# A decoder layer on one NeuronCore: the first unit of either feed-forward network reordered on three engines, and the last tile of the first down projection done bank by bank

## The reference

```python
h = swiglu(rms_norm(x, ffn1_pre_g), w_gate, w_up, w_down)     # 2048 -> 5632 -> 2048
x = x + 0.5 * rms_norm(h, ffn1_post_g)
u = rms_norm(x, mix_pre_g)                                    # one input projection
a, m = mla_attention(...), moba_attention(...)                # 8 heads each
y = concat[rms_norm(a), rms_norm(m)] @ w_out
x = x + rms_norm(y, mix_post_g)
x = x + 0.5 * rms_norm(swiglu(rms_norm(x, ffn2_pre_g), ...), ffn2_post_g)
# swiglu(x) = (silu(x @ w_gate) * (x @ w_up)) @ w_down
```

## Time and profile before

| | |
|---|---|
| median of three runs | 1758.3 us |
| profiled execution: own time / span of its instructions | 1758.18 / 1756.5 us |
| PE busy | 1737.1 us, 99% (7968 matmuls) |
| PEld busy | 1442.3 us, 82% |
| DVE busy | 1410.7 us, 80% |
| ACT busy | 1001.8 us, 57% |
| POOL busy | 65.3 us, 4% |
| granted TensorE clock, mean | 0.998 |

### The profile page before, as it was taken

How to read it: one execution, slowest core, us unless ns; L and a number is a source line. 1 busy time by engine, 2 the same in 40 slices (tenths; PEclk the granted TensorE clock), 3 DMA queues, 4 the chain that set the end, 5 groups by cost and what they waited for, 6 DMA issues and landing times. The chain is left out here.

```text
span 1756.5 us, 21394 instructions
## 1 busy us (share of the span) xinstructions
PE 1737.1 (99%) x7968; PEld 1442.3 (82%) x7968; DVE 1410.7 (80%) x1284; ACT 1001.8 (57%) x979; POOL 65.3 (4%) x99
## 2 busy tenths in 40 slices
PE   9999999999999999999999999999999999999998
PEld 8788888888888888788888878788888888888886
DVE  7888888888888888765578558888888888888887
ACT  6666565555655654543347446555666666555563
POOL 1000000000000000010000000000000000000000
PEclk9999999999999999999999999999999999999999
DMA  9777777777766554355441546777777777666453
GB/s 386 237 257 259 256 256 239 239 239 248 245 234 222 184 215 176 147 219 189 174 162 54 187 171 260 263 240 241 249 249 241 239 246 251 254 232 238 174 191 114
DMA packets 58978, 389.75 MB, mean 222 GB/s; under 512 B 6432, under 2 KB 6688, under 8 KB 16160
## 3 DMA queue, kind: packets, MB, share of 16 engines
q1 hardware_dynamic: 52720, 344.77, 50.1%
q0 software_dynamic: 6048, 44.04, 13.2%
q10 hardware_dynamic: 144, 0.04, 0.0%
HBM read 384.63 MB, written 4.19 MB: 221 GB/s over the span
## 5 line engine op out<-in xcount | busy, mean ns | idle before, releaser
L2093 PE MATMUL banks<-w_hi,act_hi 128*128 128x512 f32 (+1 forms) x1088 | 424.7, 390 | 1.1 <-DVE act_lo L1355 1.1
L2095 PE MATMUL banks<-w_hi,act_lo 128*128 128x512 f32 (+1 forms) x1088 | 421.5, 387 | 0.0
L2094 PE MATMUL banks<-w_lo,act_hi 128*128 128x512 f32 (+1 forms) x1088 | 421.2, 387 | 0.0
L1385 DVE TENSOR_TENSOR op_lo<-quads,op_hi 128x2048 fp32r<-128x2048 f32 x140 | 318.5, 2288 | 43.2 <-ACT op_hi L918 42.8
L918 ACT ACTIVATE op_hi<-quads 128x2048 fp32r<-128x2048 f32 x140 | 266.8, 1919 | 53.3 <-PE banks L2095 21.1
L2287 PE MATMUL banks<-w_hi,hid_split 128*128 128x512 f32 x992 | 275.1, 389 | 0.5 <-DVE hid_split L1616 0.5
L1374 DVE TENSOR_TENSOR w_lo<-raw,w_hi 128x2048 fp32r<-128x2048 f32 x80 | 181.3, 2287 | 78.3 <-ACT w_hi L892 78.3
L1344 DVE TENSOR_TENSOR w_lo<-raw,w_hi 128x2048 fp32r<-128x2048 f32 (+3 forms) x67 | 143.8, 2147 | 121.6 <-ACT w_hi L843 121.6
L2093 PEld LDWEIGHTS banks<-w_hi,act_hi 128*128 128x128 f32 x1088 | 204.6, 188 | 42.1 <-issue 1.8
L2095 PEld LDWEIGHTS banks<-w_hi,act_lo 128*128 128x128 f32 x1088 | 204.4, 188 | 41.7
L2094 PEld LDWEIGHTS banks<-w_lo,act_hi 128*128 128x128 f32 x1088 | 204.6, 188 | 40.0
(11 more groups left out here) (209 smaller groups left out, 2329.8 us busy)
## 6 DMA issues: line engine op xcount, KB each, us to landing
raw<-in_weights SPq DMA_DIRECT2D x203, 1024.0 KB, 5.1
quads<-in_paired SPq DMA_DIRECT2D x80, 1024.0 KB, 10.7
quads<-in_paired POOLq DMA_DIRECT2D x40, 1024.0 KB, 8.5
raw<-in_paired SPq DMA_DIRECT2D x32, 768.0 KB, 5.9
rows<-in_x SPq DMA_DIRECT2D x4, 1024.0 KB, 10.9
raw<-in_weights SPq DMA_DIRECT2D x6, 512.0 KB, 3.5
gain_row<-in_post_gains SPq DMA_DIRECT2D x3, 1024.0 KB, 6.6
raw<-in_weights SPq DMA_DIRECT2D x4, 768.0 KB, 4.1
```

What stands on the lines that cost most here:

```text
L1385: nc.vector.tensor_tensor(op_lo[:, slot, :], op_raw(op), op_hi[slot][:, :], ALU.subtract)\
L2093: nc.tensor.matmul(out_ap, hi, rhs_hi, start=start, stop=False, skip_group_check=chain)
L2094: nc.tensor.matmul(out_ap, hi, rhs_lo, start=False, stop=False, skip_group_check=chain)
L2095: return nc.tensor.matmul(out_ap, lo, rhs_hi, start=False, stop=stop, skip_group_check=chain)
```

## The change

In unit 1 of both layers, and only there:
- DVE does `multiply_hidden(stage, 1, 1)` after the low part of P6, no more ahead of `sum3`; the two joins of part1 come ahead of the low part of L4; `multiply_mixed` comes ahead of the low part of the next unit's L1.
- ACT does `keep_hidden(stage, 1, 1)` after the kept P7 and the high part of P5; the kept P5 comes ahead of the high part of L4.
- PE turns block 1 after P6, no more ahead of P7.

At the end of `DOWN1` PE does tile 1 of the last piece bank by bank: six matmuls into the first bank, a semaphore (`near_bank_done`), six into the second. ACT squares the two banks apart, in two instructions of 512 columns, so there is one more sum, one more step of the variance on POOL, and the later counts go up by one (16 to 17, 26 to 27, 28 to 29).

```diff
@@ POOL, inverse_rms
+                        if job == R_POST1 and n == parts - 1 and t == TILES - 1:
+                            sums[0] += 1
+                            pool.wait_ge(squared, sums[0])
+                            step(nc.gpsimd.tensor_scalar(var[:, job, one], sumsq[:, one, parts], c / width,
+                                                         var[:, job, one], ALU.mult, ALU.add))
@@ ACT, unit
-                keep_hidden(stage, 1 if v.first else u * 2 - 2, u * 2 - 1)
-                keep_part(stage, v, part1[:, 1, :], O_P7)
-                operand_high(stage, v, O_P5)
+                if v.first:
+                    keep_part(stage, v, part1[:, 1, :], O_P7)
+                    operand_high(stage, v, O_P5)
+                    keep_hidden(stage, 1, 1)
+                else:
...
                 keep_part(stage, v, part0[:, 1, :], O_P6)
                 operand_high(stage, v, O_P2)
-                plain_high(stage, v, L4)
-                keep_part(stage, v, part1[:, 0, :], O_P5)
+                if v.first:
+                    keep_part(stage, v, part1[:, 0, :], O_P5)
+                    plain_high(stage, v, L4)
+                else:
...
@@ ACT, in place of square_down(DOWN1, 1)
+            def square_end(stage):
+                act.wait_ge(tile0_done, DP)
+                b = down_banks(1, 0)
+                square(banks[:, b:b + 2, :].rearrange("p b n -> p (b n)"), junk[:, 0:D // 2], 0, 1)
+                act.wait_ge(near_bank_done, 1)
+                square(banks[:, down_banks(1, 1), :], junk[:, 0:BANK], 1, 1)
+                act.wait_ge(piece_used, stage + DP)
+                square(banks[:, down_banks(1, 1) + 1, :], junk[:, 0:BANK], 1, 2)
@@ DVE, unit
                 operand_low(stage, v, O_P6)
+                if v.first:
+                    multiply_hidden(stage, 1, 1)
...
-                plain_low(stage, v, L4)
+                if not v.first:
+                    plain_low(stage, v, L4)
                 dve.wait_ge(part_kept, per_unit(stage, u, 4, 4))
                 join_part(part1, 1, part1[:, 0, :])
                 dve.wait_ge(op_used, per_unit(stage, u, 3, OP_COUNT[O_P3]))
                 join_part(part1, 0, banks[:, Y_BANK, :], ALU.subtract)
+                if v.first:
+                    plain_low(stage, v, L4)
                 operand_low(stage, v, O_P4)
                 mix_block(stage, u, part1, 2, L2, 2, ALU.subtract)
-                if not last:
+                if v.first:
+                    multiply_mixed(stage, u * 2, part1, per_unit(stage, u, 4, 1))
                     plain_low(stage, unit_behind(v), L1)
-                multiply_mixed(stage, u * 2, part1, per_unit(stage, u, 4, 1))
...
@@ DVE, ahead of unit 1
-                multiply_hidden(stage, 1, 1)
                 sum3(stage, v)
@@ DVE, last scaling of DOWN1
+            def scale_last_half(t):
+                dve.wait_ge(squared, 4 + 2 * t + 1)
...
-            add_residual(R_POST1, 1, lambda t: scale_down(1, 4, t), IN)
+            add_residual(R_POST1, 1, scale_last_half, IN)
@@ PE, unit
-                turn_hidden(stage, v.u * 2 - 1)
+                if not v.first:
+                    turn_hidden(stage, v.u * 2 - 1)
                 product(stage, v, O_P7)
                 product(stage, v, O_P6)
+                if v.first:
+                    turn_hidden(stage, v.u * 2 - 1)
@@ PE, down_piece
+                    if stage == DOWN1 and n == DP - 1 and t:
+                        for k in range(2):
+                            for j in range(2):
+                                ...
+                                for lhs, rhs in ((hi, rhs_hi), (hi, rhs_lo), (lo, rhs_hi)):
+                                    mm = nc.tensor.matmul(banks[:, b + k, :], lhs, rhs[:, j, quarter(k)], ...)
+                            mm.then_inc(piece_used if k else near_bank_done, 1)
+                        continue
```

More of the change, by code:

```diff
@@ L94 @@
 G_ROWS = 4 * DC + QC + KVC
-VAR_STEPS, LAST_SUMS = 2 * (1 + 2 + 1 + 1 + 1 + 1 + 1 + OUT_BLOCKS + 1 + 1), 28
+VAR_STEPS, LAST_SUMS = 1 + 2 * (1 + 2 + 1 + 1 + 1 + 1 + 1 + OUT_BLOCKS + 1 + 1), 29
 MOBA_TAB, MLA_TAB = 3 * HD // 2, 3 * ROPE // 2
@@ L351, in build_layer @@
         last_bank_done = sem("last_bank_done")
+        near_bank_done = sem("near_bank_done")
         last_hid_ready = sem("last_hid_ready")
@@ L950, in unit @@
                 plain_high(stage, v, L3)
-                keep_hidden(stage, 1 if v.first else u * 2 - 2, u * 2 - 1)
-                keep_part(stage, v, part1[:, 1, :], O_P7)
-                operand_high(stage, v, O_P5)
+                if v.first:
[3 more added lines that the diff above has]
+                else:
+                    keep_hidden(stage, u * 2 - 2, u * 2 - 1)
+                    keep_part(stage, v, part1[:, 1, :], O_P7)
+                    operand_high(stage, v, O_P5)
                 keep_part(stage, v, part0[:, 1, :], O_P6)
                 operand_high(stage, v, O_P2)
-                plain_high(stage, v, L4)
-                keep_part(stage, v, part1[:, 0, :], O_P5)
+                if v.first:
+                    keep_part(stage, v, part1[:, 0, :], O_P5)
+                    plain_high(stage, v, L4)
+                else:
+                    plain_high(stage, v, L4)
+                    keep_part(stage, v, part1[:, 0, :], O_P5)
                 operand_high(stage, v, O_P4)
@@ L1327, in _ @@
             take_high(piece(IN))
-            square_down(DOWN1, 1)
+            square_end(DOWN1)
             take_high(piece(IN + 1))
@@ L1443, in unit @@
                 join_part(part1, 0, banks[:, Y_BANK, :], ALU.subtract)
+                if v.first:
+                    plain_low(stage, v, L4)
                 operand_low(stage, v, O_P4)
                 mix_block(stage, u, part1, 2, L2, 2, ALU.subtract)
-                if not last:
+                if v.first:
+                    multiply_mixed(stage, u * 2, part1, per_unit(stage, u, 4, 1))
                     plain_low(stage, unit_behind(v), L1)
-                multiply_mixed(stage, u * 2, part1, per_unit(stage, u, 4, 1))
+                else:
+                    if not last:
+                        plain_low(stage, unit_behind(v), L1)
+                    multiply_mixed(stage, u * 2, part1, per_unit(stage, u, 4, 1))
                 dve.wait_ge(piece_used, used(stage, u, O_P2))
@@ L1727, in scale_down @@
                                         gain_row[:, cols], ALU.mult).then_inc(y_scaled, 1)
+            def scale_last_half(t):
+                dve.wait_ge(squared, 4 + 2 * t + 1)
+                b = down_banks(1, t)
+                nc.vector.tensor_tensor(scaled[:, t, D // 2:], banks[:, b:b + 2, :].rearrange("p b n -> p (b n)"),
+                                        gain_row[:, D // 2:], ALU.mult).then_inc(y_scaled, 1)
             def down_proj(gu_stage, stage, sums_before, gain_loads):
@@ L2047, in scale_out @@
             def scale_out(n, t):
-                dve.wait_ge(squared, 16 + 2 * n + t + 1)
+                dve.wait_ge(squared, 17 + 2 * n + t + 1)
                 nc.vector.tensor_tensor(scaled[:, t, quarter(n)], result(n, t), gain_row[:, quarter(n)],
@@ L2084, in _ @@
             gate_up(GU2)
-            down_proj(GU2, DOWN2, 26, 3)
+            down_proj(GU2, DOWN2, 27, 3)
             finish()
@@ L2281, in down_piece @@
                         pe.wait_ge(end_added, added + (4 if t else 2))
+                    if stage == DOWN1 and n == DP - 1 and t:
+                        for k in range(2):
+                            for j in range(2):
+                                hi = hid_split[:, pc.split, 0, j, tile_of(t)]
+                                lo = hid_split[:, pc.split, 1, j, tile_of(t)]
+                                for lhs, rhs in ((hi, rhs_hi), (hi, rhs_lo), (lo, rhs_hi)):
+                                    mm = nc.tensor.matmul(banks[:, b + k, :], lhs, rhs[:, j, quarter(k)],
+                                                          start=False, stop=True, skip_group_check=True)
+                            mm.then_inc(piece_used if k else near_bank_done, 1)
+                        continue
                     for j in range(2):
@@ L2547, in mix_out @@
                         if i == 0 and n >= 2:
-                            pe.wait_ge(squared, 16 + 2 * (n - 1))
+                            pe.wait_ge(squared, 17 + 2 * (n - 1))
                             pe.wait_ge(y_scaled, 4 + 2 * (n - 1))
```

## The result

The changed kernel took 1775.7 us (median of 6 runs, 1775.2 to 1778.0) against 1758.5 us for the kernel before (6 runs, 1758.1 to 1759.5): a ratio of 1.010 with a 95% interval of 1.0089 to 1.0111. It is 17 us slower where 3.7 us faster was forecast. The profiled execution took 1777.99 us, its span is 1776.3 us against 1756.5, its mean granted clock 0.991 against 0.998.

A forecast was written before the change was run, and what follows sets the result against it. PE, busy 99% of 1756.5 us, was taken as the bound, so only its halts could be won. Gains 1.69 + 1.78 + 0.33 = 3.80, less 0.15, gave 3.65 us: median 1754.6 us, range 1753.2 to 1757.0.

The forecast's parts named there:

- the first stall: Unit 1, PE's wait for op_lo at P7: moving multiply_hidden behind sums and low parts gains 0.4 us.
- Gain behind L1: Unit 1, PE reaches the next P3 earlier: 1.69 us in GU1, 1.78 us in GU2.
- The joins: Unit 1, PE's wait at P2 for the joined part: joining ahead of L4's low part gains 0.45 us.
- the whole turn's stall: Unit 1, PE's turn at 91.83 waits for hid: multiply_mixed ahead of L1's low part gains 0.86 us.
- Tight places: Later waits with little cover, in unit 2 and at block 4: 0.15 us deducted, 0.6 as upper end.
- rival 1: Units 2 and 3 give back part as DMA landings don't move; P1, P7, turn stall; 1755.9 us, chance 0.25.
- The end of DOWN1: Last tile bank by bank: PE's next transposes come 0.33 us earlier, bounds 0 and 0.45.
- Rival 3: Slower: the loop falls into unit 3's pattern for good, 0.45 us in 16 more units; 1761.9 us, chance 0.03.
- Rival 2: Clock falls at GU2's start and DOWN1's end, about 0.65 us each; 1755.5 both, 1753.6 neither; chance 0.15.

The follow-up runs named there:

- hid_alone: Kernel before with only multiply_hidden(1, 1) of unit 1 moved after the low part of P6; 1776.8 us, ratio 1.0096.
- hid_back: Changed kernel with multiply_hidden(1, 1) put back ahead of sum3, all other edits kept; 1757.2 us, ratio 0.9988.
- after_sum3: As order_kept, but multiply_hidden(1, 1) stands between sum3 and sum2; 1758.9 us, ratio 0.9998.
- no_mixed: As order_kept, but multiply_mixed again behind the next L1's low part; 1757.3 us, ratio 0.9989.
- order_kept: Changed kernel with multiply_hidden, block 1's turn and keep_hidden put back; joins, early multiply_mixed and last tile stay; 1757.8 us, ratio 0.9990.
- last_tile: Kernel before with only the last tile of DOWN1 done bank by bank, units as before; 1758.8 us, ratio 0.9997.
- all_units: As order_kept, with early joins and early multiply_mixed in every unit of both layers, on ACT too; 1756.3 us, ratio 0.9983.
- warm_wait: Changed kernel plus 36 unused matmuls on PE between P1 and L1's wait for hid in unit 1; 1771.2 us, ratio 1.0066.

## Why the prediction was wrong

**The step that failed** is the first stall's: "Its hid is wanted by the turn after P6, at 65.10 + 2.85 + 2.72 = 70.67: cover 2.6 us." The turn does want it there, but PE wants the same semaphore earlier, for L1. In the kernel before hid was done at 58.22 + 0.87 = 59.09 and L1 started at 59.55: the cover was 0.46 us, and the step was moved by 9 us. I asked who reads what the moved instruction writes, and not who overwrites what it reads. The row that would have shown it was in the trace: PE's start of L1 just behind that row of DVE. And the code says it in one condition of `plain_product`. The list of PE's waits ahead of the prediction left that one out. What the runs showed in place of 2.6 us of cover is a wait of 8.47 us in GU1 and 8.44 in GU2, and 2.9 and 2.3 us for the clock on top; the move alone (hid_alone) costs 17.4 us.

**The rest of the sum**, step by step:
- Gain behind L1: forecast 1.69 in GU1; measured 1.89 with L1 late and all operands early (the books above). In hid_back, where L1 is on time, P7 starts 0.86 us late and unit 1 wins 0.83 and 0.97. In after_sum3 P7 is on time and L1 is 1.87 us late. So this move could not win the P7 stall in either place tried: the two aims (hid early for L1, sums early for P7) want the same time of DVE.
- The joins: 0.45 forecast, 0.77 in no_mixed against the kernel before, which includes what the shorter P2 wait brings forward. The early `multiply_mixed`: forecast 0.86 for the whole turn's stall, which both edits remove together; order_kept has no halt left there. Together they were forecast at 1.31 and measured 1.33 and 1.44: these two steps held.
- Tight places: I took 0.15 us and an upper end of 0.6 for both layers. In order_kept, with PE 1.4 us earlier, unit 2 loses 1.44 us; unit 3 loses 0.37 less than before, so 1.07 is the net. The mechanism was rival 1's, loads that don't land earlier when PE comes earlier, but of its three places (P1, P7, the turn) only the turn waited, for the load of L4.
- The end of DOWN1: 0.33 forecast, 0.35 in its place, with DVE and not ACT as what sets it, as forecast. Over the longer stretch of the next paragraph last_tile keeps 0.24 of it.

**The rivals.** Rival 3, the slower one, had another mechanism and did not occur. Rival 2, the clock, was near the mark for the borders between stages. The stretch from the start of unit 10 in GU1 to unit 1 of GU2 is 663.7 us in the kernel before, where the clock fell once (664.5 in hid_alone, which has the same old last tile, where it fell twice). In the kernels with the new last tile it is 663.5 to 663.6 where it fell once (hid_back, last_tile, after_sum3, no_mixed, all_units, warm_wait) and 664.4 where it fell twice (changed, order_kept): a fall there costs 0.85 us. In no_mixed it fell at the start of IN and not of GU2, in hid_back the other way round, with the same halts in both (1.36 and 1.41 us). Each of these is one profiled execution. What I did not have as a rival is the clock's fall inside unit 1, which needs the halt first, and made 17 us of what is 12 with the clock held (warm_wait).

## What to carry to other kernels

Before a step is moved later, list everyone who waits for its semaphore and for what: readers of its result, and writers who will overwrite its sources. In this kernel a PSUM bank that is read out late blocks, by its semaphore, the next sum that starts in it, and PE's first matmul into that bank is the deadline, not the consumer of the result. In a kernel where PE is the bound, the trace gives that deadline directly: look which PE instruction starts just behind the step, and treat a small distance (0.46 us here) as a dependency until the code says otherwise.

## What the runs showed of the hardware

- A halt of 8.5 us on PE cost 2.9 us more in GU1 and 2.3 in GU2 (53.53 and 52.96 us for the unit, against 50.60 and 50.62 in warm_wait), since the next matmuls ran at a granted clock of 0.50; PE resumed at 68.25 and the window from 69 to 74 us is still at 0.50. A halt of 1.7 us (after_sum3) in the same place did not lower it, while at the border before GU2 it fell after one of 1.41 us, with one of 0.56 us before it, at 1044.14. "TensorE: Matmul & The Clock Gate" of the Trainium skill, section "What's actually happening", says that the chip's watch runs freely against the kernel; the falls that change places between no_mixed and hid_back agree.
- 36 matmuls with an unused result, put into such a halt in each layer, held the clock at 1.00 and won 5.4 us over both layers. Taking the halt away (hid_back) won 19.4.
